# Turning the inverse and the keys of the RWKV stage by transposes of 64 rows into two PSUM banks

## The reference, cut to what matters

```python
def step(S, inp):
    w_t, k_t, v_t, kk_t, kka_t = inp[:5]
    S = (S * w_t[:, :, None, :]
         - jnp.einsum('bhij,bhj->bhi', S, kk_t)[..., None] * kka_t[:, :, None, :]
         + v_t[..., None] * k_t[:, :, None, :])
    y = jnp.einsum('bhij,bhj->bhi', S, inp[5]) if emit else None
    return S, y
```

## Time and profile before

| | before |
|---|---|
| median of 3 runs | 4778.45 us (4778.01 to 4781.03) |
| the profiled execution | 4780.88 us, span 4779.1 us |
| RWKV stage, 1436 to 2112 us of the span | 676 us, 28 us a group |
| PE busy over the span | 4565.8 us (96%) |
| PE busy in the stage | 622.6 of 676 us |
| DVE, ACT busy in the stage | 482.4, 436.3 us |

### The profile page before, as it was taken

One profiled execution on the slowest core, in us unless ns is written; L12 is line 12 of the kernel. 1 busy time (PEld: TensorE's weight loads), 2 busy tenths in 40 slices (PEclk: granted clock), 3 DMA queues, 4 the chain that ended last, 5 costly groups with the idle time before them and its releaser, 6 DMA issues.

```text
span 4779.1 us, 70253 instructions
## 1 busy us (share of the span) xinstructions
PE 4565.8 (96%) x29914; PEld 3230.3 (68%) x29914; DVE 2698.5 (56%) x4820; ACT 1044.8 (22%) x2337; POOL 81.2 (2%) x81
## 2 busy tenths in 40 slices
PE   7999999998999999999999999989999999989998
PEld 5556555555546676666886888545887788545886
DVE  3172445544326777744565666674656666674656
ACT  1052100002016666632002110151001010151000
POOL 0000000000000000000000000020000000020000
PEclk9998999998999999998999999989999999989999
DMA  5211122221100000012222222211222222211221
GB/s 235 110 45 53 53 106 106 106 88 53 66 18 3 3 3 3 5 51 99 89 88 74 83 76 80 96 45 71 89 88 80 79 80 80 95 47 71 88 89 44
DMA packets 27046, 339.09 MB, mean 71 GB/s; under 512 B 3024, under 2 KB 3024, under 8 KB 6896
## 3 DMA queue, kind: packets, MB, share of 16 engines
q1 hardware_dynamic: 24048, 324.51, 18.0%
q0 software_dynamic: 2688, 10.09, 0.6%
HBM read 330.40 MB, written 4.19 MB: 70 GB/s over the span
## 4 chain that ended last, share of the span: by engine, by line
PE 88%; DVE 7%; ACT 4%; issue 2%; DMA 0%; SPq 0%; ACTq 0%; DVEq 0%
PE ps L1363 46%; PE ps L1081 23%; PE ps L1153 2%; PE ps L1562 1%; PE ps L1493 1%; PE ps L1534 1%; PE ps L1545 1%; PE ps L1123 1%; ACT arena L1807 1%; PE ps L1304 1%; PE ps L1622 1%; PE ps L1431 1%; DVE arena L2879 1%; PE ps L1579 1%; DVE arena L2299 1%
## 5 line engine op out<-in xcount | busy, mean ns | idle before, releaser
L1363 PE MATMUL ps<-arena 128*128 128x256 f32 (+1 forms) x9096 | 2112.4, 394 | 15.1 <-DVE arena L2635 15.1
L1363 PEld LDWEIGHTS ps<-arena 128*128 128x128 f32 x9096 | 1734.0, 191 | 381.3 <-DVE arena L2635 17.5
L1081 PE MATMUL ps<-arena 128*128 128x512 f32 (+3 forms) x3104 | 1153.8, 533 | 10.5 <-ACT arena L1758 7.2
L1081 PEld LDWEIGHTS ps<-arena 128*128 128x128 f32 x3104 | 585.8, 192 | 566.7 <-issue 403.6
L2626 DVE TENSOR_TENSOR arena<-ps,arena 128x512 f32<-128x512 f32 (+1 forms) x250 | 157.6, 630 | 315.1 <-PE ps L1363 313.4
L2626 DVE TENSOR_TENSOR square<-ps,square 128x512 f32<-128x512 f32 (+1 forms) x145 | 99.1, 684 | 176.2 <-PE ps L1363 176.2
L2567 DVE TENSOR_TENSOR arena<-arena 128x1024 f32<-128x1024 f32 (+2 forms) x153 | 190.5, 1245 | 8.7 <-ACT arena L1758 5.5
L1948 ACT COPY square<-ps 128x512 f32<-128x512 f32 (+1 forms) x65 | 37.2, 572 | 659.1 <-PE ps L1363 591.7
L1948 ACT COPY arena<-ps 128x384 f32<-128x384 f32 (+1 forms) x35 | 18.5, 529 | 575.1 <-PE ps L1363 549.3
L2887 DVE COPY_PREDICATED arena<-const,ps 128x256 f32<-128x256 int32 x192 | 83.8, 445 | 76.4 <-PE ps L1562 70.9
L1807 ACT ACTIVATE arena<-arena,state_sum 128x256 f32<-128x256 f32 (+2 forms) x128 | 76.4, 598 | 214.6 <-DVE state_sum L2354 212.6
(11 more groups left out here) (341 smaller groups left out, 4830.7 us busy)
## 6 DMA issues: line engine op xcount, KB each, us to landing
arena<-in_panels SPq DMA_DIRECT2D x144, 2048.0 KB, 7.7
arena<-in_panels SPq DMA_DIRECT2D x9, 1536.0 KB, 6.4
arena<-in_bias POOLq DMA_DIRECT2D x8, 512.0 KB, 4.5
arena<-in_x_in SPq DMA_DIRECT2D x1, 3072.0 KB, 10.8
x_save<-arena POOLq DMA_DIRECT2D x1, 2048.0 KB, 7.5
arena<-x_save POOLq DMA_DIRECT2D x1, 2048.0 KB, 13.1
out_x<-arena SPq DMA_DIRECT2D x8, 256.0 KB, 2.2
arena<-in_panels SPq DMA_DIRECT2D x1, 1792.0 KB, 11.7
```

The costliest lines, as they stand in the source:

```text
L1081: ins = pe.matmul(dest, left(k), right(k), start=(k == 0), stop=(k == nk - 1))
L1363: ins = pe.matmul(bank[:, j * cut.side:(j + 1) * cut.side], left[:, k, j * P:(j + 1) * P], right[k], start=(k == 0), stop=(k == cut.rows - 1))
```

## The change

Four of the five turns of the inverse (k = 4, 7, 10, 13) and the turn of the keys (k = 2) are made by transposes of one head's 64 rows instead of both heads' 128. Each transpose then writes 64 columns, and those of the two heads go into two different banks: banks 2d and 2d + 1 for the inverse, banks 4 and 5 for the keys. The first turn (k = 1) stays as it was. The copies on ACT read both banks, in runs of 64 elements. In `misc_banks` the keys of a direction now take both shared banks.

```diff
--- before.py
+++ after.py
@@ -786,7 +786,8 @@
                 if k == 0:
                     use(("small", t, d), f"x_ready{d}", LEVEL_STEPS * t + 1)
                 elif k == 2:
-                    use(("turned", t, d), f"bkn_ready{d}", t + 1)
+                    for _ in range(2):
+                        use(("turned", t, d, len(plan) % 2), f"bkn_ready{d}", t + 1)
 
             def feature(p, what, d, i):
                 for k in range(2):
@@ -1515,10 +1516,13 @@
                             pe.wait_ge(sem(f"bv_ready{d}"), t + 1)
                         left_product(t, d, level)
                         if level == 0:
-                            bank = misc("turned", t, d)
+                            banks = [misc("turned", t, d, h) for h in range(2)]
+                            assert banks == [4, 5]
                             for q, e, pos, c in places(d, g):
                                 l = 2 * q + e
-                                ins = pe.transpose(ps[:, bank, l * P:(l + 1) * P], flat(bk[d][:, c // 2, 2 * e:2 * e + 2, :]), ident)
+                                for h in range(2):
+                                    ins = pe.transpose(ps[:, banks[h], l * C:(l + 1) * C],
+                                                       flat(bk[d][half(h), c // 2, 2 * e:2 * e + 2, :]), ident[half(h), half(h)])
                             ins.then_inc(sem(f"turned{d}"), one(f"turned{d}"))
                     elif part == 1:
                         pe.wait_ge(sem(f"lx_ready{d}"), LEVEL_STEPS * t + level + 1)
@@ -1526,12 +1530,20 @@
                     else:
 
                         pe.wait_ge(sem(f"z_ready{d}"), LEVELS * t + level + 2)
-                        turn_inverse(t, d, ps[:, 2 * d + 1, 2 * P:4 * P])
+                        turn_by_heads(t, d)
 
             def turn_inverse(t, d, dest):
 
                 for q in range(SIZE // 2):
                     ins = pe.transpose(dest[:, q * P:(q + 1) * P], flat(xt[t % 2][d][:, q, :, :]), ident)
+                ins.then_inc(sem(f"x_turned{d}"), one(f"x_turned{d}"))
+
+            def turn_by_heads(t, d):
+
+                for q in range(SIZE // 2):
+                    for h in range(2):
+                        ins = pe.transpose(ps[:, 2 * d + h, P + q * C:P + (q + 1) * C], flat(xt[t % 2][d][half(h), q, :, :]),
+                                           ident[half(h), half(h)])
                 ins.then_inc(sem(f"x_turned{d}"), one(f"x_turned{d}"))
 
             def left_product(t, d, level):
@@ -2009,7 +2021,7 @@
                     ins.then_inc(sem(f"v_ready{d}"), one(f"v_ready{d}"))
                 elif k == 1:
                     bank, _ = MISC[("small", t, d)]
-                    x_copy(d, ps[:, bank, 2 * P:4 * P])
+                    x_copy(d, ps[:, bank, 2 * P:4 * P].rearrange("p (q h c) -> p q h c", h=2, c=C))
                     act.wait_ge(sem(f"values{d}"), t + 1)
                     act.copy(bv[par][:, d, :, :, :].rearrange("p a b c -> p a (b c)"), both_banks(d)[:, :, 0:P]).then_inc(
                         sem(f"bv_ready{d}"), one(f"bv_ready{d}"))
@@ -2028,15 +2040,16 @@
                         ins.then_inc(sem(f"lx_ready{d}"), one(f"lx_ready{d}"))
                     elif part == 1:
                         if level == 0:
-                            bank, _ = MISC[("turned", t, d)]
                             act.wait_ge(sem(f"turned{d}"), t + 1)
-                            act.copy(flat(bkn[par][d]), ps[:, bank, :]).then_inc(sem(f"bkn_ready{d}"), one(f"bkn_ready{d}"))
+                            act.copy(bkn[par][d].rearrange("p l (h k) -> p l h k", h=2),
+                                     ps[:, 4:6, 0:SIZE * C].rearrange("p h (l k) -> p l h k", k=C)).then_inc(
+                                         sem(f"bkn_ready{d}"), one(f"bkn_ready{d}"))
                     else:
-                        x_copy(d, ps[:, 2 * d + 1, 2 * P:4 * P])
+                        x_copy(d, both_banks(d)[:, :, P:2 * P].rearrange("p h (q c) -> p q h c", c=C))
 
             def x_copy(d, src):
                 act.wait_ge(sem(f"x_turned{d}"), more(f"x_turned{d}"))
-                act.copy(x_sb[d].rearrange("p a b c -> p (a b c)"), src).then_inc(sem(f"x_ready{d}"), one(f"x_ready{d}"))
+                act.copy(x_sb[d], src).then_inc(sem(f"x_ready{d}"), one(f"x_ready{d}"))
 
             def scan(t, s, part):
                 p, g = divmod(t, GROUPS)
```

## The result

The changed kernel takes 4851.54 us (median of 4 runs, 4847.38 to 4857.74) and the kernel before 4779.74 us beside it (4 runs, 4778.01 to 4784.94): a ratio of 1.0151, with a 95% interval of 1.0139 to 1.0163. It is 1.5% slower, where 1.0% was forecast, and lies 19.5 us above the range. The profiled execution has a span of 4853.6 us, 74.5 us more than before.

What follows compares the result with a forecast made beforehand. PE was taken to bound the RWKV stage, busy 622.6 of 676 us. Waits of 11.9 + 14.4 + 15.8 + 1.2 + 3.8 = 47.1 us on 4780.88 us, less 2.4 us, gave 4825.5 us, 1.0% slower; range 4806 to 4832 us.

Steps and rivals of the forecast that it cites:

- The wait of direction 1's keys: At k = 2, PE waits for ACT's copy of direction 0's keys: 11.9, 14.4 and 15.8 us, plus 1.2 us.
- The centre wait: Direction 0's keys also wait for DVE's centre step in the 7 readout groups: 0.54 us each, 3.8 us.
- The copies: ACT's copies in runs of 64 from two banks: taken as 0, with 4 us kept for the range.
- The transposes themselves: no gain: On PE, two 64-row transposes take as long as one whole one, at 0.056 us a step: no gain.
- The rival of the overlapping halves: The two heads' transposes run fully beside each other on PE, saving 18.9 us: 4807 us, chance 0.10.
- The change of shape: the same: On PE, changing matmul form costs 0.13 us as before; 0.9 us saved and 1.0 us lost at k = 13, counted as zero.
- The rival without a drain: PE need not drain between 64 by 64 and the new form, saving 56 us: 4769.5 us, chance 0.04.
- Is anything regained?: Whether PE's later waits for ACT and DVE shrink after the stalls: taken as 0, upper bound 46.7 us.

Runs made afterwards that it cites:

- e2: Kernel before with only the new bank plan, so only the wait of the change, keys and inverse turned as before: 4853.11 us, ratio 1.0152.
- e4b: Changed kernel with 5 or 9 unused matmuls fitted into PE's stop for the copy of direction 0's keys: 4814.12 us, ratio 1.0065.
- e1: Kernel before with only the four later turns of the inverse and their copies changed, keys and bank plan as before: 4772.39 us, ratio 0.9982.
- e6: As e1, but with both transposes of the first head, then both of the second, instead of alternating heads: 4771.61 us, ratio 0.9977.
- e7: e1 plus, in places 0 and 2, keys by 64 rows, both directions side by side in two banks without the wait: 4770.72 us, ratio 0.9975.
- e5: Changed kernel with ACT copying direction 0's keys right behind direction 1's left product, ahead of the feature step: 4815.96 us, ratio 1.0072.

## Why the prediction was wrong

The sign and the place were right, the size was not: 71.8 us of loss where 47.1 were forecast. Two terms were missed, and in opposite directions: the clock, some 44 us of cost, and the shorter transposes, some 17.5 us of gain. That they partly cancel is luck; with the transposes priced right and the clock still left out, the forecast would have been 29.6 us and further off. Of its steps, in their order:

**The wait of direction 1's keys: right.** From PE's last modelled end to the next weight load it is 1.23 us in place 0 (forecast 1.19 + 0.05), 2.27 in place 1 (2.25 + 0.05) and 2.09 in place 2 (2.06 + 0.05); only group 0 has less, 1.04. e2 shows that the two waits alone, with what follows from them, make the kernel slower by 1.5%.

**The centre wait: right.** It is 0.53 us in three of the seven groups and 0.47 in the other four (forecast 0.54). All stops at the keys together are 46.1 us, where the sum had 47.1.

**The copies: right, no cost.** After against the earlier trace rows (duration min/median/max):

```profile
L2044 ACT COPY arena<-ps x48: 562/585/592, 1447.3 to 2167.5; 128x512 f32<-128x512 f32 x48
```

**"The transposes themselves: no gain": wrong.** This is a term of the sum that was mis-sized. The step took the matmuls of L1493 for the pattern, sixteen rows in 1.11 us, 0.056 us each. A transpose of that shape is not priced like them: from four (0.34 us) to eight (0.46 us) the trace shows 0.03 us each. Four of 64 rows take 0.10 us less than two of 128, and eight take 0.20 us less than four. That makes 192 x 0.10 + 48 x 0.20 = 29 us, of which the groups at full clock show less. Against before, with the stall taken out, place 0 gained 1.18 us, place 1 0.48 and place 2 0.53 (e4b's 31.49 for place 1), by this estimate 17.5 us over 8 pairs. The rest is absorbed where PE waits for ACT and DVE, as e1 shows.

The step also read one row of the trace as one matmul. The 768 rows of L1493 are two for each of 384 matmuls, as e4b's 18 rows are for 9, and the sixteen rows of L1545 are eight small matmuls and not sixteen as said further up. The old transposes stand in the trace once each (480 at L1534, as the program makes 480). But that slip is not what failed: a new transpose too is one row, and a row of L1493 remains 0.056 us. With 128 columns a row of a transpose and one of a matmul do cost the same, 0.11 us (L1521, e4b). With 64 they do not.

The rival of the overlapping halves was nearer on this term. It priced a turn's gain at 0.056 us and the keys' at 0.17, less than came. Its pace does fit: it has the last transpose start 0.11 us after the first in a turn and 0.22 in the keys, and they start 0.12 and 0.24 after it. What it lacks is that the last one lasts 0.22 us and not 0.27. Against the overlap speaks e6, which puts the two of one half behind each other and loses nothing. The starts in the trace can't decide it: in a turn they stand in pairs 3 to 8 ns apart in both orders. The Trainium skill, "TensorEngine Tiling (Array Packing)", Key Properties, says that different tiles can load and multiply in parallel. No run here shows that for the transposes. The keys were never turned in the other order, so how much of the gain is a shorter transpose and how much overlap stays open.

**"The change of shape: the same": as to the form, right.** Going to the next form still waits until 0.07 us before the modelled end, for the keys (1635.31 + 0.46 against 1635.70) and for the turn (1612.42 + 0.34 against 1612.69). The rival without a drain is out.

**"Is anything regained?": right in the main.** In e2, with the old transposes, the two old waits of the earlier trace rows are hardly changed:

```profile
PEld ps L1546 <- ACT arena L2040: 23.0, 53, 1.6
PEld ps L1535 <- DVE arena L2888: 22.8, 58, 0.8
```

They are 0.9 us shorter there. In e1, with the shorter transposes and no stall, they are 3.8 us shorter, though PE's idle time in the stage as a whole is longer (59.3 against 53.4 us). Neither alone gives the 9.3 us by which they shrank in the changed kernel; where the rest comes from is not shown.

**The term that was missing: the clock.** The step in the sum that fails is that it added the stops to work of unchanged length. By the granted clock, PE goes down to 1.2 GHz during or right behind the stop of 2.27 us in place 1 in six of seven groups of the changed kernel (10.2 us in five of them), and behind the 2.09 us of place 2 in six of seven (3.4 to 6.8 us). Behind the 1.23 us of place 0 it never does. The stage has 148.0 us of it instead of 13.7. Of these 88.7 us begin at a new stop. Another 23.9 us begin at the later stop before the left product of place 1 (1.34 to 1.62 us, in six groups), which the kernel before has as well and where it lost the clock once. The last 35.4 us lie in the first three groups: 18.3 us in group 0, in a stretch that begins 5.6 us ahead of the stage, and 17.1 us behind no new long stop. At full clock the groups give 47.1 - 17.5 = 29.6 us, so by difference, as an estimate, 43.8 of the 73.4 us are clock (44.8 with the 46.1 us that the stops measure). e4b takes 37.8 of them back by keeping PE busy in the stop, and nothing else. 109.7 us less at low clock gave 37.8 us, 0.34 us for each; in e2 it was 28.6 for 69.0, 0.41.

The Trainium skill, "TensorE: Matmul & The Clock Gate", under HAM oscillation, describes a kernel in which each wait of PE is followed by work at half clock, and prices it at half of the throttled time. That work at half clock follows a wait of PE is what these traces show too, behind stops of 2.1 to 2.3 us. The price here is below its half: by that rule, as an estimate, 134.3 us more at low clock would cost 67 us.

**What stays open.** The same stops of place 1 are mostly followed by 10.2 us of low clock in the changed kernel and by 3.4 to 6.8 us in e2, and the kernels with the shorter transposes and no new wait (e1, e6, e7) have 23.9 to 52.0 us where before has 13.7. One profile each would say little, but the mean granted clocks of all their runs agree: over the whole program some 291 us at low clock in e1 (11 runs) and 306 in e7 (9 runs), against 276 and 280 in the kernel before (21 and 17 runs); in e6 the difference is small, 286. In e1 the place is known, the stop before the left product of place 1, which the shorter transposes lengthened from 1.34 to 1.54 us. Whether its length is the cause, or the transposes themselves, no experiment separates.

## What to carry to other kernels

A buffer that two producers share now costs a wait when one of them takes all of it, and on an engine in strict order that wait is the consumer's whole queue ahead of its copy: read it from the timeline, it comes out to a few hundredths of a microsecond. Then ask what the matmul engine's clock does behind a stop of that length, since that cost nearly as much again here. And a price per row that is taken from another line should come from the same kind of operation: a matmul of the same shape was no guide to the transpose, 0.056 us a row against 0.03.

## What the runs showed of the hardware that I had not expected

- Transposes of 64 rows by 64 columns in float32 take 0.34 us for four and 0.46 us for eight, against 0.44 us for two and 0.66 us for four of 128 by 128, to the modelled end. The order of the two halves makes no difference (e1, e6).
- Stops of 2.3 us, most of them behind one of 0.5 us, brought PE's clock down to half for 3.4 to 10.2 us in six of seven groups, and stops of 2.09 us for 3.4 to 6.8, also in six of seven. Stops of 1.23 us in place 0 of the same kernel never did, but in place 1, behind one of 0.5 us, they did in four groups of e5. Where the long stops were filled with matmuls (e4b), no fall began at them.
- A float32 matmul makes two instructions in the trace, a transpose one. A matmul of 128 by 128 by 128 costs about 0.22 us and such a transpose 0.11.
